# Prompt attention: products multiplied by transposed reciprocal row sums, in place of scaled probabilities

## The reference, cut to what matters

```python
def sink_softmax(logits, sink):
    m = jnp.maximum(jnp.max(logits, axis=-1, keepdims=True), sink)
    p = jnp.exp(logits - m)
    return p / (jnp.sum(p, axis=-1, keepdims=True) + jnp.exp(sink - m))
...
    p = jax.nn.softmax(jnp.concatenate([s_meta, s_sel], axis=-1), axis=-1).astype(v.dtype)
    o = (jnp.einsum('bcgqm,bmcd->bqcgd', p[..., :META], vm)
         + jnp.einsum('bcgqn,bqncd->bqcgd', p[..., META:], vs))
```

## Time and profile before

| | |
|---|---|
| median of 3 runs | 3319.42 us (3317.32 to 3341.52) |
| profiled execution | 3321.1 us, span 3319.3 us |
| mean granted clock of PE | 0.919 |
| prompt attention of layer 0 | about 261 to 504 us of the span |
| prompt attention of layer 1 | about 1912 to 2317 us of the span |
| elsewhere | projections and feed-forward networks, attention of the 8 sample streams, index search |

### The profile page before, as it was taken

How to read it: one execution, slowest core, us unless ns; L and a number is a source line. 1 busy time by engine, 2 the same in 40 slices (tenths; PEclk the granted TensorE clock), 3 DMA queues, 4 the chain that set the end, 5 groups by cost and what they waited for, 6 DMA issues and landing times.

```text
span 3319.3 us, 46524 instructions
## 1 busy us (share of the span) xinstructions
PE 3077.3 (93%) x17607; PEld 2808.3 (85%) x17607; DVE 1565.3 (47%) x2862; ACT 717.5 (22%) x1522; POOL 1125.3 (34%) x825
## 2 busy tenths in 40 slices
PE   7968979999999999999985979888999999999998
PEld 6955659899999999987684856655989999999997
DVE  5124451544444444464597346443164444444445
ACT  3033451100000000032465235443110000000001
POOL 3213562322222222222033069875322222223221
PEclk8955799999999999999997559989999999999998
DMA  3520001111111111112011000000111111111111
GB/s 110 84 67 27 1 1 32 32 45 38 44 38 44 38 38 38 38 61 81 22 45 52 25 1 1 1 1 36 61 39 39 41 41 38 38 38 44 44 38 66
DMA packets 182945, 130.21 MB, mean 39 GB/s; under 512 B 32241, under 2 KB 172977, under 8 KB 182598
## 3 DMA queue, kind: packets, MB, share of 16 engines
q1 hardware_dynamic: 182818, 128.52, 13.4%
HBM read 112.80 MB, written 15.16 MB: 39 GB/s over the span
## 4 chain that ended last, share of the span: by engine, by line
PE 76%; POOL 10%; issue 6%; DVE 5%; SPq 1%; ACT 1%; DVEq 0%; DMA 0%; POOLq 0%; ACTq 0%
PE ps_gemm L1395 31%; PE ps_gemm L1411 17%; PE ps_gemm L1361 15%; POOL xb L1256 6%; PE ps_tr L1476 2%; POOL xa L1256 2%; PE ps_far L1673 2%; POOL comb L1285 2%; PE ps_out L1496 1%; PE ps_out L1813 1%; PE ps_near L1496 1%; DVE xl L2097 1%; PE ps_far L1603 1%; DVE m L2367 1%; DVE conv_ctx L2367 1%
## 5 line engine op out<-in xcount | busy, mean ns | idle before, releaser
L1214 POOL CAST w_hi<-w_raw 128x1024 fp32r<-128x1024 f32 x120 | 124.8, 1040 | 1130.9 <-PE ps_gemm L1395 625.6
L695 DVE TENSOR_TENSOR h<-h,ps_gemm 128x1170 f32<-128x1170 f32 x192 | 263.8, 1374 | 406.6 <-PE ps_gemm L1411 231.1
L1395 PE MATMUL ps_gemm<-xh,w_hi 128*128 128x390 f32 x1920 | 448.1, 341 | 0.0
L1395 PE MATMUL ps_gemm<-xh,w_lo 128*128 128x390 f32 x1920 | 448.1, 342 | 0.0
L1395 PE MATMUL ps_gemm<-xl,w_hi 128*128 128x390 f32 x1920 | 446.1, 340 | 0.0
L1395 PEld LDWEIGHTS ps_gemm<-xh,w_hi 128*128 128x128 f32 x1920 | 352.5, 189 | 0.0
L1395 PEld LDWEIGHTS ps_gemm<-xl,w_hi 128*128 128x128 f32 x1920 | 349.4, 189 | 0.0
L1395 PEld LDWEIGHTS ps_gemm<-xh,w_lo 128*128 128x128 f32 x1920 | 349.1, 189 | 0.0
L1217 POOL TENSOR_TENSOR w_lo<-w_raw,w_hi 128x1024 fp32r<-128x1024 f32 x120 | 287.5, 2395 | 17.4
L1361 PE MATMUL ps_gemm<-xl,w_hi 128*128 128x390 f32 (+1 forms) x1152 | 273.1, 346 | 0.0
L1256 POOL TENSOR_SCALAR xb<-xb,stats 128x144 f32<-128x144 f32 (+7 forms) x128 | 229.0, 1800 | 72.7 <-DVE stats L2190 72.6
(11 more groups left out here) (367 smaller groups left out, 4874.0 us busy)
## 6 DMA issues: line engine op xcount, KB each, us to landing
w_raw<-in_w_gate SPq DMA_DIRECT2D x44, 512.0 KB, 3.8
w_raw<-in_w_up SPq DMA_DIRECT2D x44, 512.0 KB, 3.8
w_raw<-in_w_down SPq DMA_DIRECT2D x44, 512.0 KB, 3.2
w_raw<-in_w_in_b SPq DMA_DIRECT2D x13, 512.0 KB, 3.9
w_raw<-in_w_qkv_a SPq DMA_DIRECT2D x10, 512.0 KB, 3.9
residual_park<-h SPq DMA_DIRECT2D x1, 4680.0 KB, 13.7
h<-residual_park SPq DMA_DIRECT2D x8, 585.0 KB, 7.3
out<-yt SPq DMA_DIRECT2D x9, 512.0 KB
```

Of the source, the lines that this page charges most:

```text
L695: dve.tensor_tensor(c3(h[:, m, :]), c3(h[:, m, :]), pse(j), ALU.add).then_inc(evac[j % 2], 1)
L1214: pool.tensor_copy(whi[c % 3][:], raw[c % 2][:]).then_inc(w_hi_done, 1)
L1395: mm = pe.matmul(ps[j % 2][:, m_, 0:CH], w[:, k, :], x[:, k, m_ * CH:(m_ + 1) * CH], start=(k == 0 and w is wh and x is XH), stop=(k == KT ...
```

## The change

The probabilities are no longer scaled. Instead each pair gets one more block, "rinv": two matmuls with the identity transpose the reciprocal sums, broadcast to 64 columns for each head, so that the block holds for every query (column) its reciprocal sum in all 64 rows of the head. It is evicted with the group that it closes, and DVE's `finish` multiplies the output bank by it into a buffer `o_scaled` (two of them). POOL then makes the high part (copy) and the low part (subtraction) of the output (`split_output`), where ACT and DVE did that before. The meta block is transposed over 128 columns instead of 32 and multiplied with a `vbd` of 128 rows (its rows behind the 32 are zero), so that an eviction is one copy for the whole group. PE goes through a pair's groups in twos: two groups' transposes, then two groups' products. Waits on the outputs go over from `p_out` to `p_mul`, the count of scaled outputs; the planner's loads are adapted.

```diff
@@ -158,8 +158,8 @@
         FULL = KT * T * 4
         rreg = region(4 * T + 56, [("rms_scale", [P, T], F32)],
                       [("q_rows", [P, 2, 2 * P], F32), ("opa", [P, 2, P], F32),
-                       ("vsam", [P, P], F32), ("vbd", [32, 2, P], F32), ("stats", [P, 24], F32)],
-                      [("skip_rows", [P, 2, 2 * P], F32), ("skip_opa", [P, 2, P], F32), ("kbd", [P, 32], F32)])
+                       ("vsam", [P, P], F32), ("vbd", [P, 2, P], F32), ("stats", [P, 24], F32)],
+                      [("skip_rows", [P, 2, 2 * P], F32), ("o_scaled", [P, 2, P], F32), ("kbd", [P, 32], F32)])
         R = rreg["rms_scale"]
         sc_off, off = {}, 0
         for t in range(2, QT):
@@ -450,18 +450,16 @@
             for n in range(NP):
                 t = n // 8
                 w = (272 if t else 144) if layer == 0 else width_b(t)
-                load["dve"] += 2 * (w + 230) + 450 + (layer and t >= 2) * 460 + (layer and t < 4) * 500
-                load["act"] += 2 * (0.85 * w + 470) + 275
-                blocks = [(r, i) for i in key_tiles(layer, t) for r in range(2)] + ["meta"]
+                load["dve"] += 2 * (w + 300) + 450 + (layer and t >= 2) * 460
+                load["act"] += 2 * (0.85 * w + 470)
+                blocks = [(r, i) for i in key_tiles(layer, t) for r in range(2)] + ["meta", "rinv"]
                 for b0 in range(0, len(blocks), 4):
                     part = blocks[b0:b0 + 4]
-                    nw = sum(b != "meta" for b in part)
-                    cost = {"dve": (170 + 135 * nw) * (nw > 0) + 260 * ("meta" in part),
-                            "act": (180 + 106 * nw) * (nw > 0) + 280 * ("meta" in part)}
+                    cost = {"dve": 165 + 132 * len(part), "act": 180 + 105 * len(part)}
                     who = min(cost, key=lambda e: load[e] + cost[e])
                     load[who] += cost[who]
                     groups.append({"n": n, "t": t, "blocks": part, "who": who, "j": base + len(groups),
-                                   "first": b0 == 0, "last": "meta" in part})
+                                   "first": b0 == 0, "last": "rinv" in part})
             return groups
 
         VG = [value_groups(0, 0)]
@@ -600,12 +598,12 @@
         p_min = sem("pair_row_min_done")
         p_exp = sem("pair_probs_done")
         p_rinv = sem("pair_row_sum_inverse_done")
-        p_norm = sem("pair_probs_scaled")
         p_tr = sem("pair_probs_transposed")
         p_ev = [sem("pair_probs_out0"), sem("pair_probs_out1")]
         p_pv = sem("pair_values_done")
         p_ohi = sem("pair_output_hi_done")
         p_out = sem("pair_output_lo_done")
+        p_mul = sem("pair_output_scaled")
         p_sink = sem("pair_sinks_set")
         p_comb = sem("pair_bias_plus_mask_done")
         vbd_zero = sem("meta_values_zeroed")
@@ -1154,7 +1152,7 @@
             for c in range(C_WOB + 3, C_FFB):
                 if c == C_WOB + 5:
 
-                    sp.wait_ge(p_pv, NV[2])
+                    sp.wait_ge(p_mul, 2 * NP)
                     for m in range(KT):
                         sp.dma_start(h[:, m, :], park_dram[:, m * T:(m + 1) * T]).then_inc(back[m], 16)
                 load_w(c)
@@ -1246,14 +1244,15 @@
                         pool.tensor_copy(rows.rearrange("p (g a k t) -> p g a k t", g=KV_A, a=2, t=DEC_SEQ)[r, :, p],
                                                q[r, :, c].rearrange("p (g k) t -> p g k t", g=KV_A)).then_inc(s_qrows, 1)
 
-            def norm_pair(layer, n):
-
-                t, m = n // 8, NP * layer + n
-                pool.wait_ge(p_rinv, m + 1)
-                for r in range(2):
-                    a, b = x_keys(layer, t, r)
-                    x = x_of(layer, n)[:, a:b]
-                    pool.tensor_scalar(x, x, stat(2, n, r), None, ALU.mult).then_inc(p_norm, 1)
+            def split_output(layer, n):
+
+                t, pr = divmod(n, 8)
+                m = NP * layer + n
+                o = rreg["o_scaled"][:, n % 2, :]
+                pool.wait_ge(p_mul, m + 1)
+                pool.tensor_copy(OH[:, pr, cols(t)], o).then_inc(p_ohi, 1)
+                pool.wait_ge(p_ohi, m + 1)
+                pool.tensor_tensor(XL[:, pr, cols(t)], o, OH[:, pr, cols(t)].bitcast(F32), ALU.subtract).then_inc(p_out, 1)
 
             def set_sinks(n):
 
@@ -1299,11 +1298,11 @@
                     pool.wait_ge(s_qrows, 2 * (u["b"] + 2))
                 pool.wait_ge(pe_tr, UA[n - 3]["t_end"]) if n >= 3 else pool.wait_ge(mm_done, J_WOA)
                 pool.tensor_copy(x12["xs_a"][:, n % 3, 0:1], srow[:, u["g"], 2:3]).then_inc(s_sink, 1)
-            for n in range(NP + 1):
+            for n in range(NP + LAG + 1):
                 if n < NP:
                     set_sinks(n)
-                if n >= 1:
-                    norm_pair(0, n - 1)
+                if n >= LAG + 1:
+                    split_output(0, n - LAG - 1)
             split_ffn(C_FFA, 1)
 
             def scale_rows(i):
@@ -1331,11 +1330,11 @@
             pool.wait_ge(bb_in, 16)
             pool.wait_ge(masks, 8)
             add_masks(0)
-            for n in range(NP + 1):
+            for n in range(NP + LAG + 1):
                 if n + 1 < NP:
                     add_masks(n + 1)
-                if n >= 1:
-                    norm_pair(1, n - 1)
+                if n >= LAG + 1:
+                    split_output(1, n - LAG - 1)
             split_ffn(C_FFB, 3)
             add_squares(4)
 
@@ -1467,13 +1466,19 @@
                 def transposes(g):
                     j, n, t = g["j"], g["n"], g["t"]
                     if g["first"]:
-                        pe.wait_ge(p_norm, 2 * (NP * layer + n) + 2)
+                        pe.wait_ge(p_exp, 2 * (NP * layer + n) + 2)
                     if j >= 2:
                         pe.wait_ge(p_ev[j % 2], j // 2)
                     x = x_of(layer, n)
                     for i, b in enumerate(g["blocks"]):
-                        c, rows = (meta_col(layer, t), 2 * META) if b == "meta" else (xcol(layer, t, *b), P)
-                        mm = pe.transpose(tb[j % 2][0:rows, P * i:P * (i + 1)], x[:, c:c + rows], ident[:])
+                        if b == "rinv":
+                            pe.wait_ge(p_rinv, NP * layer + n + 1)
+                            for r in range(2):
+                                mm = pe.matmul(tb[j % 2][HD * r:HD * (r + 1), P * i:P * (i + 1)],
+                                               stat(2, n, r).to_broadcast([P, HD]), ident[:], start=True, stop=True)
+                        else:
+                            c = meta_col(layer, t) if b == "meta" else xcol(layer, t, *b)
+                            mm = pe.transpose(tb[j % 2][:, P * i:P * (i + 1)], x[:, c:c + P], ident[:])
                     mm.then_inc(p_tr, 1)
 
                 def products(g):
@@ -1483,15 +1488,15 @@
                     if g["first"]:
                         single = layer and n >= 52
                         if m >= 2 or single:
-                            pe.wait_ge(p_out, m if single else m - 1)
+                            pe.wait_ge(p_mul, m if single else m - 1)
                     bank, slot, tiles = out_bank(layer, n), pt_slot(layer, j), key_tiles(layer, g["t"])
                     for i, b in enumerate(g["blocks"]):
                         p = slot[:, P * i:P * (i + 1)]
                         if b == "meta":
                             if n == 0:
                                 pe.wait_ge(vbd_in, n_vbd)
-                            mm = pe.matmul(bank[:, 0:P], meta_values(n % 8), p[0:2 * META, :], start=False, stop=True)
-                        else:
+                            mm = pe.matmul(bank[:, 0:P], meta_values(n % 8), p, start=False, stop=True)
+                        elif b != "rinv":
                             r, tile = b
                             mm = pe.matmul(bank[HD * r:HD * (r + 1), 0:P], values(n % 8, tile), p,
                                            start=(tile == tiles[0]), stop=False)
@@ -1501,10 +1506,13 @@
                     if n < NP:
                         scores(n)
                     if n >= LAG:
-                        for g in of_pair(layer, n - LAG):
-                            transposes(g)
-                            if g["j"] - 2 >= NV[layer]:
-                                products(VG[layer][g["j"] - 2 - NV[layer]])
+                        gs = of_pair(layer, n - LAG)
+                        for i in range(0, len(gs), 2):
+                            for g in gs[i:i + 2]:
+                                transposes(g)
+                            for g in gs[i:i + 2]:
+                                if g["j"] - 2 >= NV[layer]:
+                                    products(VG[layer][g["j"] - 2 - NV[layer]])
                 for g in VG[layer][-2:]:
                     products(g)
 
@@ -1796,7 +1804,7 @@
                         mm = pe.matmul(far[r][:, o_m:o_m + META], lhs[r], keys[r][:, 0:META], start=True, stop=True)
```

(34 more changed lines are left out.)

## The result

The changed kernel takes 3164.28 us (median of 4 executions, 3157.5 to 3167.48) against 3330.47 us of the kernel before beside it (3317.32 to 3349.86): ratio 0.949, 95% interval 0.944 to 0.955.

What follows compares the result with a forecast made beforehand. At full clock POOL's scaling was taken to bound, at half clock PE. Layer 0 -26.8, layer 1 -35.5 and open splits +1.6 gave -60.7 us: 3259 us predicted, range 3207 to 3315.

Steps and rivals of the forecast that it cites:

- POOL's wait, all out: PE's waits for POOL's scaling before transposes, both prompt attention stages: the whole 83 us taken out.
- another wait: Rival: transposes wait for evictions ACT reaches after an exponential, 112 pairs x 0.58 = 65 us, 3324; chance 0.12.
- The 12 us set aside for waits in layer 1: Layer 1's prompt attention from query tile t=2 on: plus 4%, 12 us, for waits that come back.
- The two matmuls at 0.30 us: Reciprocal-transposing matmuls on PE: four records a pair, 0.30 us at full clock, 0.53 at half.
- Groups in twos ... I price the order at 0.: PE's order of transposes and products: distance to the awaited eviction stays as before, so 0 us.
- 2.63 + 0.35: Layer 0 pair at full clock: PE's own work 2.63 us plus 0.35 for the additions, 3.0 rounded up.
- The clock: t=0 at half in both stages, four half-clock pairs after it.: Query tile t=0 at half clock, 29.2 us in each layer; four more half-clock pairs in layer 0, 8.5 us.
- the 9 for start and tail: Layer 0's prompt attention: 9 us for start and tail, the tail alone 9.50 at half clock before.
- more gain: Rival: clock rises in t=0 of both stages (25), no half-clock pairs (13), no waits (12): 3209; chance 0.15.
- Layer 1 from t=2 on: 308.1 us forecast: Layer 1's prompt attention from query tile t=2: 284.7 busy, 8.4 half-clock gain, 16.8 additions, 12 waits, 3 start.
- Split, evictions, sinks, masks hidden: POOL and DVE work off PE's path: hidden, except one open split at each stage's end, 0.8 us twice.
- The low clock: Rival: clock stays at half until t=2 of layer 1, +110 us in layer 0, +13 in layer 1: 3382; chance 0.09.

Runs made afterwards that it cites:

- e3: Kernel before without GpSimd's scaling of the probabilities, division by the row sums left out: 3230.34 us, 0.977 of before.
- e14: Changed kernel with one matmul of 128 stationary columns a pair in place of two of 64, GpSimd spreading the reciprocals first: 3174.19 us.
- e7: Changed kernel with eight idle 128 x 512 matmuls ahead of layer 1's attention over the cache: 3175.33 us.
- e16: Changed kernel run again unchanged, beside the narrow-meta-block variant on the same chip: 3162.18 us.
- e11: Kernel before without GpSimd's scaling (no division by the row sums) and with groups in twos: 3166.1 us.
- e10: Changed kernel without reciprocal matmuls (no division by the row sums), meta block narrow, old order of one group's transposes, then products: 3174.8 us.
- e9: Changed kernel without the two reciprocal matmuls (no division by the row sums) and with the narrow meta block, groups in twos: 3143.4 us.
- e1: Changed kernel with TensorE's old order, one group's transposes and products, then the next's: 3196.07 us, 0.969 of before.
- e15: Changed kernel with the meta block narrow as before (32 columns, 32 rows), beside the changed kernel on one chip: 3172.81 us.

## Why the prediction was wrong

Direction and main mechanism held: POOL's wait is gone, PE sets the pace, nothing took POOL's place. The size was 103 us short (-60.7 forecast, -163.6 between the two profiled spans). By its own steps:

- **POOL's wait, all out.** Right: 83 us of waits were taken out, and taking the scaling alone away gave some 77 less (e3). ACT now stands for 0.3 us in layer 0 and 2.5 in layer 1 before transposes; *another wait* did not come. The 12 us set aside for waits in layer 1 were not needed in full: from t=2 on PE idled 252.7 - 247.8 = 4.9.
- **The two matmuls at 0.30 us.** Close: 0.27 from start to start, 0.22 from the variant without them, though 0.30 was called the least. Its row, 0.59 for eight records, has a change of shape at its end, and those records start in twos as well. The records are two for each matmul, 512 for 256. The Trainium skill ("FP8 and Floating Point Precision", TensorE Precision Notes) has four passes for true float32. The forecast took a record for a pass, came to 0.59 by it and read the trace as speaking against it; that reading is wrong. At clock 1.00 a full-width record takes 0.11 us with 128 columns passing (e14, four from 400.28 to 400.72) and 0.43 with 512 (the idle matmuls of e7, ten from 1750.53 to 1754.82). That is two cycles of 2.4 GHz a column, and with two records a matmul four: an estimate from these rows, which fits the page's four.
- **"Groups in twos ... I price the order at 0."** The step that failed first. It looked only at the waits between a transpose and its eviction, and there it was right. The order acts on PE itself: fewer changes of shape. With the old order a pair of layer 0 takes 2.98 us; with the new one 2.68. Over 56 pairs that is 16.8 us, and 32 in the whole program. That 2.98 is the forecast's 2.63 + 0.35 is chance: without the wait the old order takes 2.56 (e3), and the additions cost 0.42 in it, one change of shape among them, and 0.22 in the new one. The price was in the rows: the lone meta transpose took 0.21 us beside 0.15 for one in a batch, which I read as a base for its width.
- **The clock: t=0 at half in both stages, four half-clock pairs after it.** The mechanism was right, the time too long. Layer 0: t=0 took 24.0 us, not 29.2; of the 8.5 for half-clock pairs nothing came (t=1 took 20.4 us, less than eight full pairs); and the 9 for start and tail were taken from a tail at half clock, which took 2.2 at full. Together 21 us, some 7 of them the luck of that execution: in e16 the rise came 16 us later and the stage took 182.4. In layer 1, t=0 and t=1 took 50.6 us, not 57.4. The rival *more gain* had this as its mechanism, at 0.15. What the forecast gave as its cause, no gap and more matmul, does not carry it alone: without gaps alone the profile shows 131 us at 0.50, and with neither addition, in twos, 36.
- **Layer 1 from t=2 on: 308.1 us forecast, 252.7 measured.** The order takes 13 of the 55 us (266.0 in the old order). Another 9 is the half clock that was left in the rows of before: I put it at 20 us from one stretch; the stretches at 0.50 from 1988 us on hold 41 us of busy PE, worth 17, not 8.4. Some 10 are the waits and the start that didn't come. About 7 are the wide meta block: it saves 0.06 to 0.14 us a pair from t=3 on, where 0.05 was added. The other 16 I can't split; busy time with modelled ends, taken as work, is part of it (a pair of t=5 at full clock counts 5.76 to 5.92 us busy before, and 5.70 to 5.77 from start to start without POOL's wait).
- **Split, evictions, sinks, masks hidden.** Right: the last product to the first matmul of the output projection is 1.28 us, and no wait names POOL. That the new evictions give something of their own, 23 us with the order in twos, most of it by the clock in layer 1, wasn't in the sum.
- **The low clock,** the rival on the slower side, didn't come about. The rule beside it (the Trainium skill, "TensorE: Matmul & The Clock Gate", Part 4: transposes do not count as busy for the gate as other matmuls do) can't be the whole of it here: e3 and e11 issue the same transposes and the same matmuls, differ in their order alone, and stayed at 0.50 for 131 and 32 us in their profiled executions; e10 and e9, on one chip, for 122 and 36.

One way through the whole, by medians: scaling off, -77 (before to e3); order in twos, -64 (to e11); new evictions, -23 (to e9); the two matmuls and the wide meta block, +15 to +21 (to the changed kernel's three medians). By the other way round (e3, e10, e9) evictions get 55 and the order 31: part of each gain is the same early rise of the clock, and it goes to whichever comes first.

What stays open: what decides whether a fully busy PE at 0.50 rises after 20, 36 or 131 us. The same program showed 20, 20 and 36 in three profiled executions, and 16 us of layer 1's gain have no term.

## What to carry to other kernels

Price an edit under the bound that the rest of the change leaves, not under the old one: the order of matmuls was worth nothing while POOL set the pace and 32 us once PE did. Where PE becomes the bound, count the changes of shape in its stream, put operations of one shape behind each other, and read batches from start to start, with the change at their end in mind. And where a stage ran at half clock, give the forecast both levels of it as cases of their own, for the clock carried tens of us here.

## What the runs showed of the hardware

- PE fully busy isn't PE at full clock: 131.28 us of 131.28 at 0.50 (e3), 40.00 of 40.00 after idle matmuls had lifted it and it had fallen again (e7).
- In these float32 streams a change of the stationary operand's shape cost 0.10 to 0.15 us, with no wait in the trace: two changes more, 2.98 against 2.68 us a pair (e1); one more, 2.56 against 2.46 (e10 and e9); one more, 0.14 us at t=5 (e15 and e16). Transposes behind products cost nothing of the kind where both are `128*128`.
- Two float32 matmuls with 64 stationary columns each, into two halves of a bank, cost no more than one with 128: their records start in twos, and a pair took 2.68 against 2.69 us (e14).
- At full clock a float32 record took 0.11 us with 128 columns passing and 0.43 with 512, and a matmul has two: an estimated four cycles of 2.4 GHz a column.
